# A hybrid decoder step on one core: running totals and state fading moved to ScalarE, two gathers and a wait for stores moved across a stage's seam

## The reference

```python
ckv_past = pool_ckv[page_table].reshape(DB, -1, KV_LORA)      # 256 values a token
kpe_past = pool_kpe[page_table].reshape(DB, -1, MLA_ROPE)     # 64 values a token
s_past = (jnp.einsum('bqhc,bkc->bhqk', q_lat, ckv_past)
          + jnp.einsum('bqhr,bkr->bhqk', q_pe, kpe_past))
...
p = jax.nn.softmax(s, axis=-1)
return jnp.einsum('bhqk,bkc->bqhc', p[..., :P], ckv_past) + ...
```

```python
o = (jnp.einsum('bhij,bjhe->bihe', sc, vb)
     + jnp.einsum('bihd,bhde->bihe', qb * q_dec[None, :, :, None], S))
S = S * s_dec[None, :, None, None] + jnp.einsum('bjhd,bjhe->bhde', kb * k_dec[None, :, :, None], vb)
```

## Time and profile before

| | us |
|---|---|
| median of 3 runs (2132.69 to 2141.49) | 2140.91 |
| the profiled execution | 2142.42 |
| its span in the trace | 2140.7 |
| stretch before the stage | 826 |
| the stage | 544 |
| stretch after it | 771 |
| TensorE busy over the span | 2013.7 (94%) |
| VectorE busy | 1447.5 (68%) |
| ScalarE busy | 763.0 (36%) |
| GpSimd busy | 277.1 (13%) |

### The profile page before, as it was taken

One profiled execution on the slowest core, in us unless ns is written; L12 is line 12 of the kernel. 1 busy time (PEld: TensorE's weight loads), 2 busy tenths in 40 slices (PEclk: granted clock), 3 DMA queues, 4 the chain that ended last, 5 costly groups with the idle time before them and its releaser, 6 DMA issues. The chain is left out here.

```text
span 2140.7 us, 46996 instructions
## 1 busy us (share of the span) xinstructions
PE 2013.7 (94%) x19805; PEld 1695.3 (79%) x19805; DVE 1447.5 (68%) x2517; ACT 763.0 (36%) x1488; POOL 277.1 (13%) x368
## 2 busy tenths in 40 slices
PE   7899999999999897999999989799899999999998
PEld 6899977799997775777777767578788888778886
DVE  3747655474855625998899988676677777655555
ACT  5433323342332211343334333534444554521110
POOL 1000001000001011322222222102401200000000
PEclk9999999999999998999999999899999999999999
DMA  7323345752237766999999998689928733345442
GB/s 242 111 90 107 119 148 176 234 191 86 88 118 230 248 245 237 393 379 367 365 371 384 374 355 337 219 292 353 307 50 157 123 60 104 135 146 170 147 147 89
DMA packets 205013, 454.78 MB, mean 212 GB/s; under 512 B 15328, under 2 KB 114688, under 8 KB 195600
## 3 DMA queue, kind: packets, MB, share of 16 engines
q0 software_dynamic: 49552, 252.12, 35.8%
q1 hardware_dynamic: 155264, 199.81, 28.1%
HBM read 350.00 MB, written 101.69 MB: 211 GB/s over the span
## 5 line engine op out<-in xcount | busy, mean ns | idle before, releaser
L2815 PE MATMUL sa_ps_s<-sa_turned,keep_q 128*32 128x128 f32 x5120 | 186.8, 279 | 31.1 <-DVE sa_turned L2571 25.9
L1178 PE MATMUL pj_ps<-pj_w,pj_xh_s 128*128 128x256 f32 (+1 forms) x1088 | 194.3, 282 | 0.0
L2815 PEld LDWEIGHTS sa_ps_s<-sa_turned,keep_q 128*32 128x32 f32 x5120 | 135.3, 111 | 60.3 <-DVE sa_turned L2571 37.4
L1178 PE MATMUL pj_ps<-pj_w,pj_xh 128*128 128x256 f32 (+1 forms) x960 | 174.2, 284 | 4.4 <-DVE pj_kT L873 4.4
L1178 PEld LDWEIGHTS pj_ps<-pj_w,pj_xh_s 128*128 128x128 f32 x1088 | 168.1, 190 | 0.3 <-issue 0.3
L2571 DVE STREAM_TRANSPOSE sa_turned<-sa_nat 128x2048 f32<-128x2048 f32 x64 | 147.0, 2297 | 19.6 <-DMA sa_kp<-cache_kpe,keep_index 19.4
L1178 PEld LDWEIGHTS pj_ps<-pj_w,pj_xh 128*128 128x128 f32 x960 | 150.5, 194 | 10.4 <-issue 10.4
L879 DVE TENSOR_TENSOR pj_w<-pj_raw,pj_w 128x1024 fp32r<-128x1024 f32 (+1 forms) x86 | 102.6, 1193 | 76.8 <-ACT pj_w L701 76.6
L1178 PE MATMUL pj_ps<-pj_w,pj_xl_s 128*128 128x256 f32 (+1 forms) x544 | 153.1, 281 | 0.0
L2571 DVE STREAM_TRANSPOSE sa_turned<-keep_nat 128x2048 f32<-128x2048 f32 x64 | 146.8, 2293 | 7.8 <-PEq L85 4.8
L701 ACT CAST pj_w<-pj_raw 128x1024 fp32r<-128x1024 f32 (+1 forms) x86 | 88.1, 1024 | 154.2 <-PE pj_ps L1178 84.1
(11 more groups left out here) (523 smaller groups left out, 4977.7 us busy)
## 6 DMA issues: line engine op xcount, KB each, us to landing
pj_raw<-w_in POOLq DMA_DIRECT2D x32, 1024.0 KB, 7.0
s_zn<-pj_c SPq DMA_DIRECT2D x32, 512.0 KB, 3.0
rm_z<-s_zn SPq DMA_DIRECT2D x16, 768.0 KB, 9.4
s_zt<-pj_c SPq DMA_DIRECT2D x20, 512.0 KB, 3.4
s_x<-pj_late_x SPq DMA_DIRECT2D x32, 256.0 KB, 3.7
s_k<-lp_st SPq DMA_DIRECT2D x16, 512.0 KB, 8.9
s_v<-lp_st SPq DMA_DIRECT2D x32, 256.0 KB, 4.9
s_qn<-lp_st SPq DMA_DIRECT2D x16, 512.0 KB, 5.5
```

The costliest lines, as they stand in the source:

```text
L1178: mm = pe.matmul(ps[:, bank + u, x2 * SW:x2 * SW + w], of[a][:, k, rows_at:rows_at + P], wt[:, b, k, 0:w], start=opens and (x2, k, a, b) = ...
L2815: mm = pe.matmul(ps_s[j * QR:(j + 1) * QR, s, 0:TQ * QR], q32[:, u, c, :], turned[:, s, c, j * TQ:(j + 1) * TQ, :].rearrange("p x q -> p ( ...
```

## The change

Four things:

- `add_up` on VectorE no longer updates the column of totals. ScalarE does it, in a new `add_total` behind the copy of the probabilities, as an ACTIVATE with the ratio as scale and the step's total as bias.
- The state's fading (state times constant) moves from VectorE's `new_state` to ScalarE's new `fade_state`, four ACTIVATEs ahead of the first `memory_turned`, which waits for `out_ps`. VectorE then adds the product in PSUM in one operation over all heads.
- Steps 2 and 3 are gathered in `SamplePrepare.pool`, into four more kept buffers below those of steps 0 and 1. The wait for block 0's z in GpSimd's loop goes.
- The wait for the gate tiles' stores moves from the end of `project` to the start of the next stage: SyncE waits ahead of its first load, GpSimd ahead of its first memset.

```diff
+        keep.st_out = st_out
...
-                for j in range(2):
-                    sp.wait_ge(st_out[j], 16 * SLOTS // 4)
...
+        def gates_stored(eng):
+            for j in range(2):
+                eng.wait_ge(keep.st_out[j], 16 * SLOTS // 4)
...
+                gates_stored(sp)
                 load(0)
...
+                gates_stored(pool)
                 pool.memset(half[:, :], -0.5).then_inc(power_ok, 1)
                 pool.memset(state[:, :, :], 0.0).then_inc(state_clear, 1)
                 for g in range(1, STEPS + DEEP):
-                    if g == 3:
-                        pool.wait_ge(z_in[0], 32)
-                    if 1 < g < STEPS:
-                        if g >= DEEP:
-                            pool.wait_ge(pv_ps, g - DEEP + 1)
+                    if DEEP <= g < STEPS:
+                        pool.wait_ge(pv_ps, g - DEEP + 1)
                         gather(pool, t, index, g, nat[g % DEEP], kp[g % DEEP], nat_in[g % DEEP])
...
-                    dve.scalar_tensor_tensor(acc[:, u, KVL:KVL + 1], acc[:, u, KVL:KVL + 1], ratio[:, s:s + 1], total[:, s:s + 1],
-                                             ALU.mult, ALU.add)
...
                 def new_state(b):
-                    dve.wait_ge(out_ps, b + 1)
+                    dve.wait_ge(faded_ok, b + 1)
                     dve.wait_ge(st_ps, b + 1)
-                    for h in range(HEADS):
-                        last = dve.scalar_tensor_tensor(state[:, h, :], state[:, h, :], S_DEC[h], bank_b[:, h, :], ALU.mult, ALU.add)
-                    last.then_inc(state_ok, 1)
+                    dve.tensor_tensor(state[:, :, :], state[:, :, :], bank_b[:, :, :], ALU.add).then_inc(state_ok, 1)
...
+                def add_total(g):
+                    u, s = g // PER_SET, g % 2
+                    act.wait_ge(exp_ok, g + 1)
+                    if g == 0:
+                        act.wait_ge(acc_in, 16 * QUADS)
+                    else:
+                        act.wait_ge(total_ok, g)
+                    of = acc[:, u, KVL:KVL + 1]
+                    act.activation(of, of, ACT.Identity, bias=total[:, s:s + 1], scale=ratio[:, s:s + 1]).then_inc(total_ok, 1)
+
+                def fade_state(b):
+                    act.wait_ge(out_ps, b + 1)
+                    for h in range(HEADS):
+                        last = act.activation(state[:, h, :], state[:, h, :], ACT.Copy, scale=S_DEC[h])
+                    last.then_inc(faded_ok, 1)
...
                     if begun(g, 3) is not None:
+                        fade_state(begun(g, 3))
                         memory_turned(begun(g, 3), 0)
...
                         copy_probs(g - 1)
+                        add_total(g - 1)
...
+            pool.wait_ge(self.mo_ps, 2)
+            pool.wait_ge(self.ret_out[0], 16)
+            gather(pool, t, keep.index, 2, keep.nat2, keep.kp2, keep.rows2_in)
+            pool.wait_ge(self.q32_ok, 1)
+            pool.wait_ge(self.low_ps, 1)
+            pool.wait_ge(self.kq_ok, 8)
+            pool.wait_ge(self.moT_ps, 1)
+            gather(pool, t, keep.index, 3, keep.nat3, keep.kp3, keep.rows3_in)
             pool.wait_ge(self.cats_ok, 3)
```

More of the change, by code:

```diff
@@ L272, in project @@
         c_out = [r.sem(f"c_out{j}") for j in range(4)]
-        st_out = [r.sem(f"st_out{j}") for j in range(2)]
+        st_out = [nc.alloc_semaphore(f"keep_st_out{j}") for j in range(2)]
         op_in = {n: r.sem(f"op_in_{n}") for n in FULL}
@@ L2382, in sample_attention_and_retention @@
         acc = r.sb("acc", [P, SETS, VW])
-        r.sems.extend([keep.rows_in, keep.rows1_in])
-        nat = [keep.nat, keep.nat1] + [r.sb(f"nat{k}", [P, TPP, KVL]) for k in range(2, DEEP)]
-        kp = [keep.kp, keep.kp1] + [r.sb(f"kp{k}", [P, TPP, ROPE]) for k in range(2, DEEP)]
+        r.sems.extend(keep.st_out)
+        r.sems.extend([keep.rows_in, keep.rows1_in, keep.rows2_in, keep.rows3_in])
+        nat = [keep.nat, keep.nat1, keep.nat2, keep.nat3]
+        kp = [keep.kp, keep.kp1, keep.kp2, keep.kp3]
         turned = r.sb("turned", [P, 2, CH, TPP, QR])
@@ L2407, in sample_attention_and_retention @@
          p_ps, p_ok, pv_ps, acc_ok, fin_dve, fin_pe, fin_act, next_kv_in, next_k_in, next_q_in, next_w_in, square_ok, mean_ok,
-         next_ok, w_hi) = [
+         next_ok, w_hi, total_ok, faded_ok) = [
             r.sem(n) for n in ("late_in acc_clear acc_in chain t_ok s_ps low_ok exp_ok "
                                "p_ps p_ok pv_ps acc_ok fin_dve fin_pe fin_act next_kv_in next_k_in next_q_in next_w_in square_ok mean_ok "
-                               "next_ok w_hi").split()]
+                               "next_ok w_hi total_ok faded_ok").split()]
         sums = r.sb("sums", [P, 2, BATCH4])
@@ L2415, in sample_attention_and_retention @@
         nat_in = [r.sem(f"nat_in{k}") for k in range(DEEP)]
-        nat_in[1] = keep.rows1_in
+        nat_in[1:] = keep.rows1_in, keep.rows2_in, keep.rows3_in
         m = Room(nc, ctx, "rm")
@@ L2456, in sample_attention_and_retention @@
         cat_r_out, cat_m_out = m.sem("cat_r_out"), m.sem("cat_m_out")
+        if nc.sbuf_base > keep.edge:
+            raise ValueError("the sample's memory and its first rows")
         S_DEC = [float(np.float32((1.0 - 2.0 ** (-5.0 - h)) ** P)) for h in range(HEADS)]
+        def gates_stored(eng):
+            for j in range(2):
+                eng.wait_ge(keep.st_out[j], 16 * SLOTS // 4)
         def begun(g, after):
@@ L2655, in _ @@
                 dve.wait_ge(acc_ok, STEPS)
+                dve.wait_ge(total_ok, STEPS)
                 dve.tensor_copy(last_low[:, :], low[:, 0, :]).then_inc(fin_dve, 1)
@@ L2995, in __init__, with below @@
         self.rows1_in = nc.alloc_semaphore("keep_rows1_in")
+        edge = Count(nc.sbuf_top)
+        def below(name, shape):
+            return nc.alloc_sbuf_tensor_at(f"keep_{name}", shape, F32, offset=edge.up(-4 * shape[1] * shape[2]))
+        self.nat2, self.kp2 = below("nat2", [P, TPP, KVL]), below("kp2", [P, TPP, ROPE])
+        self.nat3, self.kp3 = below("nat3", [P, TPP, KVL]), below("kp3", [P, TPP, ROPE])
+        self.edge = edge.at
+        self.rows2_in = nc.alloc_semaphore("keep_rows2_in")
+        self.rows3_in = nc.alloc_semaphore("keep_rows3_in")
 class SamplePrepare:
```

## The result

The changed kernel takes **2149.58 us** in the median of 20 runs, beside 2141.85 us for the kernel before: ratio 1.0039, interval 1.0025 to 1.0053, so 8 us slower (5 to 11). All ratios here are estimated over all executions and are not the quotients of the two medians. I had forecast 2137.5 us and a range up to 2148; the result lies above it. The profiled execution took 2151.18 us (span 2149.4), 8.8 us more than that of before.

The account below looks back on a forecast made before the run. A loop of gathers, VectorE (90% busy) and TensorE (92%), DMA share 0.96, was taken as the bound; 2142.42 - 2.2 - 2.6 + 0.8 + 0 = 2138.4, or 2136.9 on the median's footing; forecast 2137.5 us, range 2127.5 to 2148.

Parts of the forecast that it names:

- Seam: Opening of the paged-cache stage: with the gate tiles' last store awaited later, it starts 2.2 us earlier (1.5 to 2.6).
- Steps 2 and 3 early: Start of the stage: VectorE no longer waits 1.06 and 1.55 us for these two gathers, 2.6 us saved.
- Tail: Last block of the stage: nothing absorbs the later state, so normalisation and everything after come 0.8 us later (0.5 to 1).
- Sizes of the fading: State update: four ACTIVATEs on ScalarE take 0.9 us; VectorE's addition starts 1.0 us after TensorE's last product (0.9 to 1.25).
- The steady part: Four-step cycles between the stage's start and tail: later state and shorter other steps net to 0 us (-3 to +8).
- Full absorption in about 11 of 15 cycles: Steady cycles: landing waits swallow the 0.3 us delay in 11, giving back 0.1 each; the other four pay 0.3.
- Rival 3: State step's hand-over TensorE, ScalarE, VectorE not absorbed, delaying next gathers: 0.55 to 0.9 us a cycle, 2145 to 2150; chance 0.24.
- Rivals 1, 2 and 4: 1: VectorE's whole relief appears, 2127.4 us, chance 0.13; 2: bound by bytes, 2124.5, 0.05; 4: early gathers don't help, 2140, 0.08.
- Rival 2: Stage bound by bytes: taking 5.24 MB of gathers out is worth 14.2 us, giving 2124.5 us; chance 0.05.

Follow-up runs that it names:

- `total_only`: The kernel before with only the running totals moved to ScalarE; fading, gathers and seam as they were: ratio 0.9990 (0.9973 to 1.0006) against the kernel before.

## Why the prediction was wrong

- **Seam** (-2.2): right, 2.0 us.
- **Steps 2 and 3 early** (-2.6): the two waits went, but only 1.6 us came. I gave step 4 a landing of 9 us "on emptier queues"; its second gather landed about 11.8 us after the first was issued (836.30 to 848.15), and it waited 0.98 us.
- **Tail** (+0.8): right, 0.9 to 1.0.
- **Sizes of the fading**: right. 0.91 us for four ACTIVATEs (0.9 taken), 0.98 us to the addition (1.0 taken). The total on ScalarE costs 0.39 us each, hidden as assumed: `total_only` shows no loss.
- **The steady part** (0): this step failed. "Full absorption in about 11 of 15 cycles" did not hold in the changed kernel: I had sized the steady part at 0 and it measured +12.4 us in the profiled execution. Landing waits took up 6.4 us, while VectorE's wait ahead of the state grew by 18.1. Taking the fading out of the hand-over brought 9.3 us back. Rival 3 named that step and its number fits (2145 to 2150), but not its reason: no gather landed later (median 9.9 us against 10.3), and TensorE waited longer for VectorE's turned rows instead. That its number fits is in part luck, since it had no term for the waits for instructions, and at three other placings the same hand-over cost nothing that can be told.
- What I had not seen is why it got so dear. I read TensorE as 92% busy with idle time to spare. The "issue" waits are in the profile of the kernel before as well; with 6.0 us of supply for a block that is worked off in 6.4, they say that TensorE runs close to the end of its instructions all through the stage. In block 0 one can follow it: TensorE waits 2.54 us at a block's end, drops to half clock for 3.4 us, ends its state products late and passes that on through the fading to VectorE, which stood 3.88 us. All six kernels with early gathers and no surplus instructions wait at this same instruction (1.7 to 2.8 us), the kernel before does not; that it comes from the faster start is my reading, not shown. At another placing of the blocks the same kernel lies between 4.3 us below and 3.0 us above the kernel before, in the mean of the three 0.9 us below, where I had forecast 3.4 below.
- **Rivals 1, 2 and 4**: VectorE's relief turned into waits. Rival 2 had a point: with fewer bytes both kernels gain 20 us, so the transfers do bind, but not through the two gathers moved.

What stays open: why a given placing is bad, and so what share of the 8 us is the hand-over's and what share the placing's. I can name the places and the waits, but not forecast from the order of the instructions which block end will meet a full queue.

## What to carry to other kernels

An operation moved to an idle engine is not free when it comes to stand between two engines that hand to each other: look at the room between releaser and use (0.03 to 0.26 us here), and if there is none, compute ahead into a second tile. (Here that gave the loss back and no clear gain: 0.9 us below the kernel before.) Waits of TensorE for "issue" next to full DMA queues are a resource of their own; look whether they lie multiples of 256 instructions apart, all that the engine executes counted. Their sum does not tell what they cost. Before a difference of 0.5% is put down to an edit, shift the program by 64 or 128 instructions and time it again: here that moved the same kernel by 13 us, from 8.4 above (5 to 11) to 4.3 below (1 to 8).

## What the hardware showed that I had not expected

- A block of 256 TensorE instructions needs one 16384-byte packet. Beside gathers at 0.94 share it starts 3.7 us after the block ahead of it was begun (3.1 to 3.3 at 0.72), takes 1.0 us, and a TensorE that waits for it resumes 1.1 to 1.6 us after its end.
- Of the six waits of this kind over 2 us in the changed kernel, four had 3.4 us or more at 1.2 GHz beginning within 1.1 us of their end (after the one of 2.54 us, pairs of products took 0.63 us instead of 0.39); those of 2.70 us (to 887.04) and 2.36 us (to 939.07) had none.
- With 32 surplus matmuls (128 instructions) a kernel was 9.9 us faster, with a margin of 5 us.
